# Scores of the forgetting attention in two products instead of three: queries and keys doubled in their rows, bias rows masked by head

## The chip, the cores and the metric

The kernel runs on one core of one Trainium2 chip. The metric is the device time of one execution in microseconds (us). The kernel before takes 1488.74 us, the median of three runs (1486.61 to 1490.23).

## What is computed

One layer of a decoder: a mixer of three branches (a latent attention, a forgetting attention, a state-space layer), gated and summed, and then a convolved feed-forward network, for 1024 tokens of width 1024 in float32. The change is in the forgetting attention, which has 4 heads of 64 columns. For a query i and a key j <= i its score is a product of normed rows plus a difference of running sums:

```python
q_fox = rms_norm(fq.reshape(bsz, seq, N_FOX_HEADS, FOX_HEAD_DIM), fox_q_norm_g)
k_fox = rms_norm(fk.reshape(bsz, seq, N_FOX_HEADS, FOX_HEAD_DIM), fox_k_norm_g)
log_f = jax.nn.log_sigmoid((f_logit + fox_f_bias).astype(jnp.float32))
cum_log_f = lax.cumsum(log_f, axis=1)
# in causal_block_attention, per block of 128 queries:
s = jnp.einsum('bqhd,bkhd->bhqk', qb, kb).astype(jnp.float32) * scale
s = s + (c_q - c_k)
p = jax.nn.softmax(jnp.where(mask, s, NEG_INF), axis=-1)
```

## The kernel before, in words

The program runs in four blocks: norm and input projection, `stage_fox` (this attention), `stage_mla` (the other attention), and the rest. The order on each engine is written out by hand, and semaphores join the engines. Float32 operands are multiplied in parts: each is split in a rounded high part (type fp32r) and a low part, the rest, and a product is the sum high x high, high x low, low x high, so three matrix products for one.

The projection of the gates for the third stage needs no result of the attentions, so `GateFill` spreads its 24 units of 48 products (128x512) over all stages as filling for TensorE (L540). ScalarE splits the high part of its weights (L564) and copies the results out (L575), GpSimd makes the low part (L586), once VectorE (L592), and SyncE loads and stores. In `stage_fox` the units before the first head cover the preparation: VectorE makes the running sums of log f (up to L1016), squares and norms of queries and keys (L1003 to L1027), GpSimd the power -1/2 (L955). It writes each token's 64 query or key columns and two bias columns side by side (`aug`, 66 columns): one and c for queries, -c and one for keys, so that the product over 66 rows holds the bias.

Then `Attention` runs 4 heads of 8 steps. Step i handles 128 queries against 128(i+1) keys. On TensorE (`tensor`, with `score`, `turn` and `values`) a step is:

- `score` of the step after next (L699, and L701 for the causal mask), three products for each 512 keys; it may start when ScalarE has read the same buffer (exp of this step);
- in steps 3, 5, 6 and 7, `turn` of one half of the next head's queries or keys (L685), which makes rows of the 66 columns, in a buffer of two banks;
- when the probabilities of this step are normed, their transposes (L680) into the same two banks, four blocks to a fill, with gate products between;
- every second step, `values` (L718).

A fill of a bank may begin when the low part of the fill before last is made. For each fill ScalarE writes the high part (`split_hi`, L780) and VectorE the low part (`split_lo`, L861). ScalarE also makes the exponentials (L790) and a copy of the outputs (L804), VectorE the maximum (L848), the reciprocal and the norm (L854, L856), and the sum of outputs (L867). The opening of the first head (`OPENING`) is: the two query fills, 6 gate products, the two key fills, 9 gate products, the first score.

## Time and profile before

| | us |
|---|---|
| Median of three runs (lowest to highest) | 1488.74 (1486.61 to 1490.23) |
| Span of the profiled execution, first to last instruction | 1487.9 |
| TensorE matmuls busy, of the span | 1443.8 (97%) |
| VectorE busy | 1003.4 (67%) |
| ScalarE busy | 651.2 (44%) |
| GpSimd busy | 127.2 (9%) |
| `stage_fox`, from its first gate product to its last product | about 172.7 to 343.9 |

The profiled execution has no time of its own beside its span; the span lies 0.8 us under the median. A busy TensorE is not one at its peak: matmuls overlap, their recorded length holds the latency of the array, and so what a product costs is read from the distance of starts. PEld is the weight load of TensorE, which runs beside the products. "Idle before" in a timeline row is put in brackets, with what ended it.

### The profile page before, as it was taken

Reading aid. Unit: us, or ns where it says so; the run is one execution under the profiler, and the core shown is the slowest. Engines: PE = TensorE matmul, PEld = TensorE weight load, DVE = VectorE, ACT = ScalarE, POOL = GpSimd, SP = SyncE. Lnnn points to the kernel's source line nnn. Section 1 sums busy time; section 2 is a strip of 40 time slices with the busy share of each in tenths; the row PEclk is TensorE's granted clock in tenths of the full one; section 3 lists DMA queues with packets and bytes.
Section 4 is the critical chain, followed back from the end, with each engine's and each line's share of the span. In section 5 each row is a group of like instructions: output and inputs, shape, how many; then the busy total and the mean of one; then the engine's idle time right before and its main releaser. Section 6 shows DMA issues by size and latency. Waiting matters only on the chain.

```text
span 1487.9 us, 18903 instructions
## 1 busy us (share of the span) xinstructions
PE 1443.8 (97%) x7090; PEld 1209.9 (81%) x7090; DVE 1003.4 (67%) x1378; ACT 651.2 (44%) x1054; POOL 127.2 (9%) x104
## 2 busy tenths in 40 slices
PE   7999999999999999998999999999999999999999
PEld 6999987777878777886788888888888888888887
DVE  5212366765676766856855688877877777679786
ACT  6230235554435553125632265555555555444332
POOL 1000141001420003011200000000000000000000
PEclk9999999999999999999999999999999999999999
DMA  7201231104021103226672222222222221891222
GB/s 255 67 1 75 64 92 43 37 29 147 26 84 48 33 29 100 73 64 219 211 262 85 71 62 95 85 85 79 77 86 85 85 86 49 313 388 71 85 79 78
DMA packets 129941, 148.93 MB, mean 100 GB/s; under 512 B 11002, under 2 KB 94893, under 8 KB 129581
## 3 DMA queue, kind: packets, MB, share of 16 engines
q1 hardware_dynamic: 129664, 147.67, 30.0%
q8 instruction: 56, 0.92, 0.3%
q14 instruction: 32, 0.26, 0.1%
q10 hardware_dynamic: 189, 0.08, 0.0%
HBM read 110.83 MB, written 36.31 MB: 99 GB/s over the span
## 4 chain that ended last, share of the span: by engine, by line
PE 52%; DVE 6%; issue 1%; ACT 1%; DMA 1%; POOL 0%; DVEq 0%; ACTq 0%; SPq 0%
PE ps L1876 28%; PE ps L2183 5%; PE ps L2185 5%; PE ps L2184 4%; PE ps L2753 2%; PE ps L2754 2%; PE ps L2755 2%; PE ps L540 2%; DVE plain_arena L2279 1%; PE ps L2272 1%; DMA plain_arena<-in_w_branch 1%; PE ps L2785 0%; DVE plain_arena L2543 0%; DMA plain_arena<-in_w_out 0%; DVE plain_arena L1047 0%
## 5 line engine op out<-in xcount | busy, mean ns | idle before, releaser
L1876 PE MATMUL ps<-split_arena 128*128 128x512 f32 x1320 | 306.8, 389 | 0.0
L540 PE MATMUL ps<-split_arena 128*128 128x512 f32 x1152 | 293.2, 402 | 6.0 <-PEq L1117 2.1
L1876 PEld LDWEIGHTS ps<-split_arena 128*128 128x128 f32 x1320 | 247.5, 188 | 51.4 <-issue 0.3
L540 PEld LDWEIGHTS ps<-split_arena 128*128 128x128 f32 x1152 | 210.2, 190 | 48.2 <-issue 8.2
L2059 ACT ACTIVATE down_ops<-down_all 128x1024 fp32r<-128x1024 f32 x77 | 81.5, 1061 | 115.5 <-PE ps L2185 115.3
L1876 PE MATMUL ps<-up_b,split_arena 128*128 128x512 f32 x528 | 126.5, 389 | 0.0
L2078 DVE TENSOR_TENSOR down_ops<-down_all,down_ops 128x1024 fp32r<-128x1024 f32 x77 | 94.1, 1223 | 46.2 <-ACT down_ops L2059 46.0
L2183 PE MATMUL ps<-down_ops 128*128 128x512 f32 x308 | 119.9, 389 | 0.5 <-DVE down_ops L2078 0.5
L2185 PE MATMUL ps<-down_ops 128*128 128x512 f32 x308 | 119.8, 389 | 0.0
L2184 PE MATMUL ps<-down_ops 128*128 128x512 f32 x308 | 119.8, 389 | 0.0
L1876 PEld LDWEIGHTS ps<-up_b,split_arena 128*128 128x128 f32 x528 | 99.1, 188 | 20.6
L327 PE MATMUL ps<-split_arena 128*128 128x426 f32 (+1 forms) x256 | 93.1, 364 | 2.3 <-DVE split_arena L213 2.3
L328 PE MATMUL ps<-split_arena 128*128 128x426 f32 (+1 forms) x256 | 92.0, 359 | 0.0
L329 PE MATMUL ps<-split_arena 128*128 128x426 f32 (+1 forms) x256 | 91.7, 358 | 0.0
L586 POOL TENSOR_TENSOR split_arena<-plain_arena,split_arena 128x1024 fp32r<-128x1024 f32 x23 | 63.7, 2768 | 323.2 <-ACT split_arena L564 323.2
L465 DVE COPY plain_arena<-ps 128x426 f32<-128x426 f32 (+6 forms) x28 | 10.3, 406 | 104.0 <-PE ps L329 104.0
L848 DVE TENSOR_REDUCE stat<-ps 128x1 f32<-128x128 f32 (+3 forms) x64 | 48.3, 755 | 44.2 <-PE ps L701 44.2
L2272 PE MATMUL ps<-split_arena 128*128 128x512 f32 x288 | 68.5, 394 | 6.6 <-DVE plain_arena L2279 3.7
L575 ACT ACTIVATE plain_arena<-ps 128x512 f32<-128x512 f32 x48 | 28.6, 597 | 102.7 <-DMA scr_gate<-plain_arena 68.1
L1804 DVE TENSOR_TENSOR split_arena<-up_s,split_arena 128x512 fp32r<-128x512 f32 x88 | 60.4, 687 | 18.2 <-ACT split_arena L1749 18.2
L2272 PEld LDWEIGHTS ps<-split_arena 128*128 128x128 f32 x288 | 53.4, 188 | 21.4 <-POOL split_arena L2261 8.5
L2183 PEld LDWEIGHTS ps<-down_ops 128*128 128x128 f32 x308 | 57.8, 188 | 12.7 <-DVE down_ops L2078 0.9
(359 smaller groups left out, 2510.8 us busy)
## 6 DMA issues: line engine op xcount, KB each, us to landing
plain_arena<-in_w_in SPq DMA_DIRECT2D x24, 512.0 KB, 4.2
scr_gate<-plain_arena SPq DMA_DIRECT2D x48, 256.0 KB, 2.0
plain_arena<-scr_gate SPq DMA_DIRECT2D x24, 512.0 KB, 4.3
plain_arena<-in_w_up SPq DMA_DIRECT2D x22, 512.0 KB, 5.1
up_raw<-in_w_up SPq DMA_DIRECT2D x22, 512.0 KB, 4.7
scr_act<-plain_arena SPq DMA_DIRECT2D x22, 512.0 KB, 2.7
down_all<-scr_act SPq DMA_DIRECT2D x18, 512.0 KB, 8.8
down_all<-in_w_down SPq DMA_DIRECT2D x18, 512.0 KB, 10.3
```

Of the source, the lines that this page charges most:

```text
L327: nc.tensor.matmul(o, hi, wh, start=(k == 0), stop=False)
L328: nc.tensor.matmul(o, hi, wl, start=False, stop=False)
L329: mm = nc.tensor.matmul(o, lo, wh, start=False, stop=(k == KD - 1))
L540: mm = nc.tensor.matmul(m.ps[:, self.banks[half], :], w[:, k, :], src[:, k, h * BANK:(h + 1) * BANK], start=(j == 0), stop=(j == self.PER_ ...
L586: self.m.nc.gpsimd.tensor_tensor(self.w_lo[u % 2], self.raw, f32(self.w_hi[u % 2]), ALU.subtract).then_inc(self.lo, 1)
L1876: mm = nc.tensor.matmul(o, self.w[j][w][:, k, :], self.h[j][k][h], start=(j in self.OPENS and k == 0 and n == 0), stop=(k == self.HK - 1 a ...
L2059: self.m.nc.scalar.activation(self.hi_of[n % 3], self.pair(n)[0], ACT.Copy).then_inc(self.hi, 1)
L2078: self.m.nc.vector.tensor_tensor(self.lo_of[n % 3], self.pair(n)[0], f32(self.hi_of[n % 3]), ALU.subtract).then_inc(self.lo, 1)
L2183: nc.tensor.matmul(o, a_hi[:, cut], b_hi, start=(k == 0 and j in self.OPENS), stop=False, skip_group_check=True)
L2184: nc.tensor.matmul(o, a_hi[:, cut], b_lo, start=False, stop=False, skip_group_check=True)
L2185: mm = nc.tensor.matmul(o, a_lo[:, cut], b_hi, start=False, stop=(k == HF - 1), skip_group_check=True)
L2272: mm = nc.tensor.matmul(proj_ps[u % 2][:, cut], w[:, k, :], src[:, 2 * n + k, cut], start=(k == 0 and w is hi and src is m.br_hi), stop=(k ...
```

## The change

The queries' transposed tile `q_t[0]` now holds 128 rows: the high part in rows 0 to 63 and the low part in rows 64 to 127; `k_t[0]` holds the keys' high part twice. One product over these 128 rows is high x high plus low x high. The second product, over 80 rows, is the queries' high part (`q_t[1]`, written by its own copy, L950 in the new numbering) with the keys' low part, and 16 bias rows: four for each head (ones, and the high and low part of c), the same for the queries of all heads, while those of the keys are multiplied before each head by a column that is one for the head's four rows and zero elsewhere (`head_bias`, on GpSimd). So that a transpose gives the rows twice, each token's 64 columns are written twice (`rows`, doubled by three ScalarE copies, L1061). The bias columns of all heads are transposed once, in the middle of the preparation (L1075), and four ScalarE copies put them in place (L1057). The causal mask's product stays. The other attention keeps three products. Buffers of the stage move to other addresses.

```diff
+    def score_pairs(self, tokens, keys):
+        (q_hi, q_lo), (k_hi, k_lo) = ([a[0:self.kd, cut] for a in t] for t, cut in ((self.q_t, tokens), (self.k_t, keys)))
+        return (q_hi, k_hi), (q_hi, k_lo), (q_lo, k_hi)
+
+    def ready_for_score(self, pe, h, half):
+        pe.wait_ge(self.lo, self.at["k", h, half] + 1)
...
-            for n, (x, y) in enumerate(((0, 0), (0, 1), (1, 0))):
-                nc.tensor.matmul(S[:, a:b], self.q_t[x][0:kd, i * P:(i + 1) * P], self.k_t[y][0:kd, a:b], start=(n == 0),
-                                 stop=(n == 2 and b < keys))
+            pairs = self.score_pairs(slice(i * P, (i + 1) * P), slice(a, b))
+            for n, (x, y) in enumerate(pairs):
+                nc.tensor.matmul(S[:, a:b], x, y, start=(n == 0), stop=(n == len(pairs) - 1 and b < keys))
...
-        self.ready(pe)
         for what, n in zip("qk", OPENING):
+            self.ready(pe, what)
...
+    def score_pairs(self, tokens, keys):
+        q_both, q_low = self.q_t
+        k_both, k_low = self.k_t
+        return (q_both[:, tokens], k_both[:, keys]), (q_low[0:self.LOW, tokens], k_low[0:self.LOW, keys])
+
+    def ready_for_score(self, pe, h, half):
+        pe.wait_ge(self.lo, self.at["k", h, half] + 1)
+        pe.wait_ge(self.q_kept, 2 * h + half + 1)
+        pe.wait_ge(self.bias, h + 1)
+
+    def split_hi(self, act, f):
+        x = self.fills[f]
+        if x[0] == "p":
+            super().split_hi(act, f)
+            return
+        what, h, half = x
+        cut, bank = slice(half * BANK, (half + 1) * BANK), self.m.ps[:, 4 + f % 2, :]
+        act.wait_ge(self.turned, f + 1)
+        if h:
+            act.wait_ge(self.scores, TT * (h - 1) + (4 if what == "q" and half == 0 else TT))
+        to = self.q_t if what == "q" else self.k_t
+        A = self.m.nc.scalar.activation
+        A(to[0][:, cut], bank, ACT.Copy).then_inc(self.hi, 1)
+        if what == "q":
+            A(to[1][0:FD, cut], bank[0:FD], ACT.Copy).then_inc(self.q_kept, 1)
+
+    def split_lo(self, dve, f):
+        x = self.fills[f]
+        if x[0] == "p":
+            super().split_lo(dve, f)
+            return
+        what, h, half = x
+        cut, bank = slice(half * BANK, (half + 1) * BANK), self.m.ps[:, 4 + f % 2, :]
+        dve.wait_ge(self.hi, f + 1)
+        if what == "q":
+            dve.wait_ge(self.q_kept, 2 * h + half + 1)
+            hi, lo, rows = self.q_t[0], self.q_t[0], slice(FD, 2 * FD)
+        else:
+            hi, lo, rows = self.k_t[0], self.k_t[1], slice(0, FD)
+        self.m.nc.vector.tensor_tensor(lo[rows, cut], bank[rows], f32(hi[rows, cut]), ALU.subtract).then_inc(self.lo, 1)
+
+    def head_bias(self, pool, h):
+
+        if h:
+            pool.wait_ge(self.scores, TT * h)
+        pool.wait_ge(self.fill.lo, self.fill.split)
+        r = slice(FD, self.LOW)
+        self.m.nc.gpsimd.tensor_scalar(self.k_t[1][r, :], f32(self.master[r, :]), self.of_head[r, h:h + 1], None, ALU.mult).then_inc(self.bias, 1)
+        pool.wait_ge(self.bias, h + 1)
+
+
...
-    def ready(pe):
-        pe.wait_ge(prep, 1)
+    def ready(pe, what):
+        pe.wait_ge(doubled, 1 if what == "q" else 3)
+        pe.wait_ge(bias_out, 4)
...
-            fill.gpsimd(pool, FOX_UNITS - 1)
+            mask = att.of_head
+            nc.gpsimd.memset(mask, 1.0).then_inc(const, 1)
+            pool.wait_ge(const, 4)
+            nc.gpsimd.affine_select(out=mask, in_=mask, compare_op=ALU.is_ge, fill=0.0, base=-FD, pattern=[[-4, FH]], channel_multiplier=1).then_inc(const, 1)
+            pool.wait_ge(const, 5)
+            nc.gpsimd.affine_select(out=mask, in_=mask, compare_op=ALU.is_ge, fill=0.0, base=FD + 3, pattern=[[4, FH]], channel_multiplier=-1).then_inc(const, 1)
+            fill.gpsimd(pool, FOX_PREP - 1)
+            pool.wait_ge(const, 6)
+            pool.wait_ge(bias_out, 4)
+            for h in range(H):
+                att.head_bias(pool, h)
+                fill.gpsimd(pool, 1)
...
-            fill.scalar(act, FOX_PREP * UNIT - UNIT // 2)
+            fill.scalar(act, 2 * UNIT)
+            for half in range(2):
+                cut = slice(half * BANK, (half + 1) * BANK)
+                act.wait_ge(cols_turned, half + 1)
+                for to, r in ((q_t[1], 64), (att.master, 96)):
+                    nc.scalar.activation(to[FD:FD + 16, cut], m.ps[r:r + 16, 4 + half, :], ACT.Copy).then_inc(bias_out, 1)
+            fill.scalar(act, FOX_PREP * UNIT - UNIT // 2 - 2 * UNIT)
+            for n, (first, last) in enumerate(((0, FH), (FH, FH + 1), (FH + 1, 2 * FH))):
+                act.wait_ge(prep, min(n, 1) + 1)
+                nc.scalar.activation(rows[:, :, first:last, 1, :], rows[:, :, first:last, 0, :], ACT.Copy).then_inc(doubled, 1)
             att.scalar(act)
...
-            fill.tensor(pe, (FOX_PREP - 1) * UNIT - sum(OPENING))
+            fill.tensor(pe, UNIT + UNIT // 2)
+            pe.wait_ge(cols_done, 1)
+            for t in range(TT):
+                tr = nc.tensor.transpose(m.ps[0:112, 4 + t // 4, t % 4 * P:(t % 4 + 1) * P], bias_cols[:, t, :], m.ident[:])
+                if t % 4 == 3:
+                    tr.then_inc(cols_turned, 1)
+            fill.tensor(pe, (FOX_PREP - 1) * UNIT - sum(OPENING) - UNIT - UNIT // 2)
...
-            step(V.memset(aug[:, :, 0:FH, FD:FD + 1], 1.0))
-            step(V.tensor_copy(aug[:, :, 0:FH, FD + 1], cum))
-            step(V.tensor_scalar(aug[:, :, FH:2 * FH, FD], cum, -1.0, None, ALU.mult))
-            step(V.memset(aug[:, :, FH:2 * FH, FD + 1:FD + 2], 1.0))
+            step(V.memset(bias_cols, 1.0))
+            step(V.tensor_copy(cum_hi, cum))
+            of_q, of_k = (bias_cols[:, :, at:at + 16].rearrange("p t (h n) -> p t h n", n=4) for at in (64, 96))
+            step(V.tensor_copy(of_q[:, :, :, 0], f32(cum_hi)))
+            step(V.tensor_tensor(of_q[:, :, :, 1], cum, f32(cum_hi), ALU.subtract))
+            step(V.tensor_scalar(of_k[:, :, :, 2], f32(cum_hi), -1.0, None, ALU.mult))
+            V.tensor_tensor(of_k[:, :, :, 3], f32(cum_hi), cum, ALU.subtract).then_inc(cols_done, 1)
...
-            step(V.tensor_tensor(aug[:, :, 0:FH, 0:FD], sqv[:, :, 0:FH, :],
-                                 gq.unsqueeze(1).unsqueeze(1).to_broadcast([P, TT, FH, FD]), ALU.mult))
-            V.tensor_tensor(aug[:, :, FH:2 * FH, 0:FD], sqv[:, :, FH:2 * FH, :],
+            V.tensor_tensor(rows[:, :, 0:FH, 0, :], sqv[:, :, 0:FH, :],
+                            gq.unsqueeze(1).unsqueeze(1).to_broadcast([P, TT, FH, FD]), ALU.mult).then_inc(prep, 1)
+            V.tensor_tensor(rows[:, :, FH:2 * FH, 0, :], sqv[:, :, FH:2 * FH, :],
                             gk.unsqueeze(1).unsqueeze(1).to_broadcast([P, TT, FH, FD]), ALU.mult).then_inc(prep, 1)
```

ScalarE, from the gate copies ahead of the first head to the first head's splits (`scr_gate` copies are L575; `ps` is PSUM, `split_arena` holds the split parts, `plain_arena` plain float32). Before:

```order
L575 ACTIVATE plain_arena<-ps 128x512 [waits gate_stored,gate_mm] x2
L564 ACTIVATE split_arena<-plain_arena 128x1024 [waits gate_mm,gate_w_in]
L575 ACTIVATE plain_arena<-ps 128x512 [waits gate_stored,gate_mm]
L780 ACTIVATE split_arena<-ps 66x512 [waits fox_turned] x4
L575 ACTIVATE plain_arena<-ps 128x512 [waits gate_stored,gate_mm]
```

Now:

```order
L575 ACTIVATE plain_arena<-ps 128x512 [waits gate_stored,gate_mm] x2
L564 ACTIVATE split_arena<-plain_arena 128x1024 [waits gate_mm,gate_w_in]
L575 ACTIVATE plain_arena<-ps 128x512 [waits gate_stored,gate_mm]
L1061 ACTIVATE plain_arena<-plain_arena 128x8x4x64 [waits fox_prep]
L1061 ACTIVATE plain_arena<-plain_arena 128x8x64 [waits fox_prep]
L1061 ACTIVATE plain_arena<-plain_arena 128x8x3x64 [waits fox_prep]
L948 ACTIVATE split_arena<-ps 128x512 [waits fox_turned]
L950 ACTIVATE split_arena<-ps 64x512
L948 ACTIVATE split_arena<-ps 128x512 [waits fox_turned]
L950 ACTIVATE split_arena<-ps 64x512
L948 ACTIVATE split_arena<-ps 128x512 [waits fox_turned] x2
L575 ACTIVATE plain_arena<-ps 128x512 [waits gate_stored,gate_mm]
```

Three copies of 2048, 512 and 1536 columns stand between the last gate copy and the first split, and each query split is two instructions.

TensorE, the opening of the first head, as a difference (- before, + now):

```order
-L685 MATMUL ps<-ident,plain_arena 66x128 [waits fox_prep]
-L685 MATMUL ps<-ident,plain_arena 66x128 x7
+L686 MATMUL ps<-ident,plain_arena 128x128 [waits fox_bias_out,fox_doubled]
+L686 MATMUL ps<-ident,plain_arena 128x128 x7
 L540 MATMUL ps<-split_arena 128x512 x6
-L685 MATMUL ps<-ident,plain_arena 66x128 [waits fox_lo]
-L685 MATMUL ps<-ident,plain_arena 66x128 x3
-L685 MATMUL ps<-ident,plain_arena 66x128 [waits fox_lo]
-L685 MATMUL ps<-ident,plain_arena 66x128 x3
+L686 MATMUL ps<-ident,plain_arena 128x128 [waits fox_lo,fox_bias_out,fox_doubled]
+L686 MATMUL ps<-ident,plain_arena 128x128 x3
+L686 MATMUL ps<-ident,plain_arena 128x128 [waits fox_lo]
```

The transposes give 128 rows, those of the queries wait for the first doubling copy and those of the keys for the third, and nothing between them moved.

ScalarE, steps 4 and 5 of the first head, where the second query half of the next head is split (`fox_pt` is the transposed probabilities). Before:

```order
L804 ACTIVATE plain_arena<-ps 64x512 [waits fox_pv]
L780 ACTIVATE split_arena<-ps 66x512 [waits fox_scores,fox_turned]
L780 ACTIVATE fox_pt_1385<-ps 128x4x128 [waits fox_pv,fox_turned]
L780 ACTIVATE fox_pt_1385<-ps 128x2x128 [waits fox_pv,fox_turned]
L790 ACTIVATE plain_arena,stat<-ps,stat 128x1024 [waits fox_recip,fox_turned,fox_negmax]
```

Now:

```order
L812 ACTIVATE plain_arena<-ps 64x512 [waits fox_pv]
L948 ACTIVATE split_arena<-ps 128x512 [waits fox_scores,fox_turned]
L950 ACTIVATE split_arena<-ps 64x512
L788 ACTIVATE fox_pt_1386<-ps 128x4x128 [waits fox_pv,fox_turned]
L788 ACTIVATE fox_pt_1386<-ps 128x2x128 [waits fox_pv,fox_turned]
L798 ACTIVATE plain_arena,stat<-ps,stat 128x1024 [waits fox_recip,fox_turned,fox_negmax]
```

The copy of the queries' high part (L950) stands between the split of the query fill and that of the probabilities.

## Rows read from the trace of the kernel before

**Rows 1.** The page: the span, and each engine's busy time and instructions.
```profile
span 1487.9 us, 18903 instructions
...
PE 1443.8 (97%) x7090; PEld 1209.9 (81%) x7090; DVE 1003.4 (67%) x1378; ACT 651.2 (44%) x1054; POOL 127.2 (9%) x104
```

**Rows 2.** By stretch: length, busy PE, PEld, DVE, ACT, POOL, granted clock, DMA share, GB/s.
```profile
172.00:219.00 47.00, 46.70 (x217) 38.59 (x216) 31.62 (x54) 15.98 (x21) 20.32 (x7) 1.00 0.36 107
219.00:343.00 124.00, 119.33 (x729) 97.39 (x728) 81.77 (x166) 68.03 (x148) 9.61 (x4) 1.00 0.12 37
```

**Rows 3.** Timeline of PE, second head: start, length, line, out<-in, shape, count.
```profile
253.41 0.91 PE L699 MATMUL ps<-split_arena 66*128 66x512 f32 x3
254.16 0.23 PE L701 MATMUL ps<-maskb,identb 128*128 128x128 bf16 x1
...
255.85 1.15 PE L699 MATMUL ps<-split_arena 66*128 66x512 f32 x6
256.83 0.23 PE L701 MATMUL ps<-maskb,identb 128*128 128x128 bf16 x1
...
266.93 1.61 PE L699 MATMUL ps<-split_arena 66*128 66x512 f32 x6
268.38 0.23 PE L701 MATMUL ps<-maskb,identb 128*128 128x128 bf16 x1
...
276.66 0.49 PE L699 MATMUL ps<-split_arena 66*128 66x128 f32 x3
```

**Rows 4.** Timeline of PE, last gate products before the first head.
```profile
204.63 9.46 PE L540 MATMUL ps<-split_arena 128*128 128x512 f32 x41
213.93 1.04 PE L685 MATMUL ps<-ident,plain_arena 128*66 128x128 f32 x8
...
219.13 0.45 PE L699 MATMUL ps<-split_arena 66*128 66x128 f32 x3
```

**Rows 5.** Timeline of ACT, first stage and opening of the first head.
```profile
178.00 3.63 ACT L964 ACTIVATE plain_arena<-plain_arena 128x4096 f32<-128x4096 f32 x1 [0.88 <-DMA scr_u<-plain_arena]
181.53 2.17 ACT L966 ACTIVATE split_arena<-plain_arena 128x512 fp32r<-128x512 f32 x4
...
213.07 0.60 ACT L575 ACTIVATE plain_arena<-ps 128x512 f32<-128x512 f32 x1 [1.16 <-DMA scr_gate<-plain_arena]
...
214.56 1.08 ACT L780 ACTIVATE split_arena<-ps 66x512 fp32r<-66x512 f32 x2 [0.90 <-PE ps L685]
```

**Rows 6.** Timeline of ACT, steps 0 and 1 of the second head.
```profile
253.67 0.28 ACT L780 ACTIVATE fox_pt<-ps 128x128 fp32r<-128x128 f32 x1 [3.01 <-PE ps L718]
...
255.48 0.60 ACT L804 ACTIVATE plain_arena<-ps 64x512 f32<-64x512 f32 x1
```

**Rows 7.** Timeline of PEld, step 2 of the second head.
```profile
257.65 0.31 PEld L680 LDWEIGHTS ps<-ident,plain_arena 128*128 128x128 f32 x3 [0.50 <-DVE plain_arena L856]
```

**Rows 8.** Timelines of ACT, DVE and PE, steps 5 and 6 of the second head.
```profile
269.08 0.60 ACT L780 ACTIVATE split_arena<-ps 66x512 fp32r<-66x512 f32 x1 [0.96 <-PE ps L685]
...
269.79 0.68 DVE L861 TENSOR_TENSOR split_arena<-ps,split_arena 66x512 fp32r<-66x512 f32 x1
...
272.14 1.02 DVE L861 TENSOR_TENSOR fox_pt<-ps,fox_pt 128x512 fp32r<-128x512 f32 x2
...
272.88 0.63 PE L685 MATMUL ps<-ident,plain_arena 128*66 128x128 f32 x4 [0.86 <-DVE fox_pt L861]
```

**Rows 9.** POOL, groups of the whole span, shapes apart: count, busy us, mean ns.
```profile
L586 POOL TENSOR_TENSOR split_arena<-plain_arena,split_arena 128x1024 fp32r<-128x1024 f32 x23 | 63.7, 2768 | 323.2 <-ACT split_arena L564 323.2
...
L955 POOL TENSOR_TENSOR statb<-stat,plain_arena 128x64 f32<-128x64 f32 x1 | 10.9, 10933 | 8.2 <-DVE stat L1004 8.2
```

**Rows 10.** Timelines of DVE and POOL in the preparation of the first attention.
```profile
203.27 4.37 DVE L1025 TENSOR_TENSOR plain_arena<-plain_arena,rowg 128x2048 f32<-128x2048 f32 x1
207.67 2.29 DVE L1027 TENSOR_TENSOR plain_arena<-plain_arena,rowg 128x2048 f32<-128x2048 f32 x1
...
201.55 3.94 POOL L586 TENSOR_TENSOR split_arena<-plain_arena,split_arena 128x1024 fp32r<-128x1024 f32 x1 [2.77 <-ACT split_arena L564]
```

## Prediction of the time after the change

> **What bounds the kernel now.** I read the page first: TensorE's products are busy 97% of the span, the next engine 67% [rows 1]. The stretches of this stage say the same at the full clock: 46.70 of 47 us in the preparation, 119.33 of 124 in the four heads, where VectorE has 81.77 and ScalarE 68.03 [rows 2]. So the stage lasts as long as TensorE's queue, and time taken from it comes back unless something ends a wait there later. TensorE's recorded lengths overlap, so its small waits hide in "busy": I went through one head in the timelines and looked for places where it is held by another engine. There are two kinds: in step 2 its weight load waits 0.50 us for the norm [rows 7], and before the key fill of step 6 it waits 0.86 us for a low part of probabilities [rows 8]. What a third product less returns depends on whether it stands behind the event that starts such a chain, or within it.
>
> **What is removed.** 48 products, one of three for each 512 keys or fewer. The three cost, from first start to the mask's start, 1.45 us at 3 x 1024 columns, 0.98 us at 3 x 640 and 0.75 us at 3 x 512 [rows 3]: 0.47 to 0.51 ns a column. A head has 4608 key columns, so a head saves between 2.17 and 2.35 us, taken as 2.23, by step 0 to 7: 0.06, 0.13, 0.19, 0.25, 0.33, 0.37, 0.42, 0.48. Four heads: 8.9 us. The new products have 128 and 80 rows where the old have 66. The gate products have 128 rows and 512 columns, and 41 of them start within 9.30 us, 0.227 us each [rows 4], no more than the 0.23 to 0.24 of the old ones; rows cost nothing. The Trainium skill speaks against this in "TensorE: Matmul & The Clock Gate", Part 3, The mechanism: a weight load overlaps a running product only when their row groups differ. By that rule each product of 128 rows would pay its load as well. The gate products all use the same 128 rows and still keep 0.227 us, so the trace disagrees, and the measurement decides.
>
> **What is added before the first head.** Eight transposes of 112 columns on TensorE, 0.10 us each by the eight of the first query fills, 1.04 us with the last one's latency of 0.27 [rows 4]: 0.8 us. Four copies of 16x512 on ScalarE, at 0.54 us (two splits in 1.08 us [rows 5]) 2.2 us, while ScalarE is busy 15.98 of 47 us [rows 2] and stands waiting for the store of the gates; hidden. The longer VectorE part (a fill of 896 columns and two more small operations, 0.7 to 1.4 us) fits in what VectorE has free (31.62 of 47 us busy [rows 2]; it waits for GpSimd's power), and GpSimd's mask column is three small operations; both hidden. The gate split that VectorE makes is late by as much, with a bound of 0.9 us if it carries through the loads to ScalarE's last gate copy.
>
> Not hidden is the doubling. It stands on ScalarE behind the gate copy at 213.07 [rows 5], and I let that copy start 0.2 later for the eight transposes, 213.27. Then, step by step: the copy 0.54; three copies of 4096 columns together at the price of the square of 4096, 3.63 [rows 5], and two more starts, 0.2: 217.6. The queries' first split and its new twin 1.08: 218.7. VectorE's low part 0.7 [rows 8]: 219.4; meanwhile the second half's split and twin end at 219.8, its low part at 220.5. The second key fill is turned after that, 4 x 0.11: 220.95. Nine gate products 9 x 0.227: 223.0, and 0.2 for the hand-overs: the first score starts at 223.2 instead of 219.13 [rows 4]. **The start costs 4.1 us.** Below it lies 2.6, if the doubling overlaps half with the 6 and 9 gate products; above it 8.8, if copies in pieces of 64 columns cost twice a plain row (+3.8) and the 0.9 of the loads comes on top.
>
> **What is added in the heads.** The twin copy of each query half, 0.54 us on ScalarE, stands between split and low part. In step 3 it moves the low part of the fill, the norm and the next transposes, which TensorE reaches just as late: 0. In step 5 it counts. Take the end of the score of step 7, about 268.6, as origin: the split starts at +0.5 (269.08), the low part at +1.2 (269.79), the low part of the probabilities at +3.5 (272.14), and TensorE waits for it until +4.3 (272.88, 0.86 idle) [rows 8]. VectorE works through from the one to the other. With the twin the low part starts at +1.6, so TensorE goes on at +4.7: 0.42 us lost in heads 0 to 2, none in head 3, which prepares no next head. Bounds: 0, and 0.54 at both halves.
>
> GpSimd's bias product for the next head may start when step 7's score is done, 268.61, and is needed at the next head's first score, 276.66 [rows 3]: 8.05 us of cover. No row shows a GpSimd product with a scalar. The nearest is the low part of 1024 columns, 2.40 us where nothing disturbs it (2.77 on the mean [rows 9]), and I take that: 0. The upper end is the power, 10.93 us for 64 columns [rows 9]. Two more waits before each score cost nothing while TensorE's queue is ahead.
>
> **What of the 8.9 us comes back.** In the heads with an output copy at step 1 (1 to 3) a chain starts when `values` has ended, 253.6: ScalarE's split of step 0 at 253.67, the gate weights, the exp, the output copy at 255.48 [rows 6], VectorE's sum and the norm (L856), and only then TensorE's transposes at 257.65, for which it waits 0.50 [rows 7]. Scores of steps 3 and 4 (0.25 and 0.33) run beside this chain: lost. So is step 1 (0.13), which stands before a key fill that VectorE holds. Steps 0, 2, 5, 6 and 7 lie before the origins of the chains and move them: 0.06 + 0.19 + 0.37 + 0.42 + 0.48 = 1.52. Less the twin: 1.10 for heads 1 and 2, 1.52 for head 3. Head 0 has no output copy at step 1 and keeps 0.58 more: 1.68. Sum 1.68 + 2.20 + 1.52 = 5.4 us.
>
> **The sum.** 5.4 - 4.1 = 1.3 us less than the profiled span: 1486.6 of 1487.9. The median of the runs lies 0.8 above that span, so I forecast 1487.4 us. A difference under 0.2%, 3.0 us, can't be told from no change here.
>
> **Rivals.**
> - *All of it comes back.* TensorE's 97% speaks for it; the waits of 0.50 and 0.86 us against. If the chains shrink with the products and the twin is covered: 8.9 - 4.1 = 4.8, 1483.9 us. Chance 0.22.
> - *The start costs its upper end.* The doubling runs in 64-column pieces and ScalarE's gate copy comes late. For it: everything there hangs on one engine in order. Against: the square runs on plain rows at 0.89 ns a column, and the splits of the values, which are 512 columns in pieces of 64, take 0.54 us each (four in 2.17 [rows 5]), as one of plain rows. 8.8 instead of 4.1: 1492.1. It turns the sign over 0.2% from a start of 8.4 on. Chance 0.11.
> - *GpSimd's bias product is slower than its cover* (slower than before). Place: between the last score of a head and the first of the next. At the power's 10.93 us each of three heads waits 2.9 us: 8.6 us, 1496.0. It decides from 8.05 us on. Against it: an elementwise operation of 1024 columns took 2.4. A weaker form needs only 2.8 us: while GpSimd reads, VectorE's operations with both inputs in SBUF stand still. This case shows it: the key and the query rows are the same product of 2048 columns, 2.29 us alone and 4.37 with GpSimd's low part beside it, which itself took 3.94 [rows 10]. VectorE's operations in the 2.8 us after the score read PSUM. That is how the Trainium skill has it ("SBUF — State Buffer", Who interferes with whom: an exclusive lock, taken by two SBUF inputs and not by one), and the trace agrees with the lock. Chance 0.05.
> - *Two products last as long as three*, because 128 rows cost more than 66. Then only the costs stay: 4.1 + 3 x 0.42 = 5.4 us, 1494.1. Rows 4 speak against it. Chance 0.03.
>
> **Numbers.** The forecast has 0.59. The range takes in the first rival with a little spread, and most of the way to the second: 1483.4 to 1491.2; 0.1 lies on each side. Faster by over 0.2%, below 1485.8: the 0.22 and a tail of the forecast (a start of 2.6 gives 1485.9), 0.27. Slower, above 1491.7: the last three rivals without the mild half of the second, 0.14. The same: 0.59.
>
> **What would show it.** After: first score about 4 us later against the start of the stage; three copies of 3.8 us in all on ScalarE ahead of it; scores of step 7 at 0.97 us to the mask; the four heads together about 5 us shorter than their 124; the wait of step 2 grown from 0.5 to about 1.1 us, the one of step 6 from 0.86 to about 1.3; the bias product near 2.4 us. I am wrong if step 2's wait has not grown, if the start is off by over 1 us, or if the time moved outside this stage.

## The result, and the profile after

| | before | after |
|---|---|---|
| Median of the runs (lowest to highest) | 1488.59 us (1486.61 to 1490.23, 5) | 1494.91 us (1493.63 to 1496.82, 5) |
| Ratio, with its 95% interval | | 1.0044 (1.0033 to 1.0055) |
| Span of the profiled execution (its own time after: 1494.63) | 1487.9 us | 1492.9 us |
| Start: stage's first long gate group to first score | 43.65 us | 51.86 us |
| Heads: first score to the gate products behind the last head | 123.64 us | 120.80 us |
| From there to the end of the span | 1145.1 us | 1145.4 us |

The change made the kernel slower, by 0.33 to 0.55%. The forecast was 1487.4 us, a tie, in a range up to 1491.2; it was wrong. In the profiles the time moved only inside this stage (8.2 - 2.8 = 5.4 us of it; the rest is within 0.6 us), and both terms of the sum are off in the same direction: the start costs 8.2 us where 4.1 were forecast, and the heads return 2.8 us where 5.4 were. "Start" and "heads" are used in this sense from here on.

The page after the change, the lines that answer to [rows 1]:

```profile
span 1492.9 us, 18903 instructions
...
PE 1438.4 (96%) x7050; PEld 1203.0 (81%) x7050; DVE 1004.7 (67%) x1380; ACT 660.6 (44%) x1069; POOL 143.8 (10%) x111
```

TensorE lost 40 instructions (48 products less, 8 transposes more) and 5.4 us of busy time, and the span grew by 5.0. The busy time of GpSimd grew by 16.6 us. By stretch, after (length, busy PE, PEld, DVE, ACT, POOL, clock, DMA share, GB/s), for [rows 2]:

```profile
172.00:227.00 55.00, 48.90 (x226) 38.86 (x224) 30.77 (x56) 23.03 (x31) 30.25 (x11) 1.00 0.30 91
227.00:348.00 121.00, 112.73 (x679) 89.95 (x679) 82.65 (x166) 70.79 (x154) 18.07 (x7) 1.00 0.12 38
```

Before, TensorE had 0.3 us free in the preparation; now 6.1, at a granted clock of 1.00 in both. So the start isn't slower products but waiting. TensorE's timeline shows where (start, length, line, shapes, count, and in brackets the wait before it):

```profile
174.88 8.86 PE L540 MATMUL ps<-split_arena 128*128 128x512 f32 x38 [0.29 <-PEq L265]
...
209.41 8.06 PE L540 MATMUL ps<-split_arena 128*128 128x512 f32 x33 [2.04 <-POOL split_arena L586]
219.57 1.09 PE L686 MATMUL ps<-ident,plain_arena 128*128 128x128 f32 x8 [2.10 <-ACT plain_arena L1061]
220.42 1.64 PE L540 MATMUL ps<-split_arena 128*128 128x512 f32 x6
223.31 0.63 PE L686 MATMUL ps<-ident,plain_arena 128*128 128x128 f32 x4 [1.25 <-DVE split_arena L965]
...
226.74 0.33 PE L708 MATMUL ps<-split_arena 128*128 128x128 f32 x2
```

First 2.04 us for GpSimd's low part of a gate weight, which nobody had to wait for before; then 2.10 us for the doubling; then 1.25 us for the opening's low parts, behind the copies of the queries.

Why GpSimd is late stands in its own timeline, after, with VectorE's of the same time. They answer to [rows 10]:

```profile
198.12 0.10 POOL L1031 MEMSET cidx<- 128x4 f32 x1
198.29 4.39 POOL L1033 TENSOR_SCALAR_AFFINE_SELECT cidx<-cidx 128x4 f32<-128x4 f32 x1
202.75 2.26 POOL L1035 TENSOR_SCALAR_AFFINE_SELECT cidx<-cidx 128x4 f32<-128x4 f32 x1
204.97 4.39 POOL L586 TENSOR_TENSOR split_arena<-plain_arena,split_arena 128x1024 fp32r<-128x1024 f32 x1
```

```profile
198.20 4.43 DVE L1126 TENSOR_TENSOR plain_arena<-plain_arena,statb 128x4096 f32<-128x4096 f32 x1 [2.96 <-POOL statb L1029]
202.66 2.29 DVE L1128 TENSOR_TENSOR plain_arena<-plain_arena,rowg 128x2048 f32<-128x2048 f32 x1
204.87 2.28 DVE L1130 TENSOR_TENSOR plain_arena<-plain_arena,rowg 128x2048 f32<-128x2048 f32 x1
```

Two selects over 4 columns took 4.39 and 2.26 us, and each ends when a VectorE product with two SBUF inputs ends: 198.20 + 4.43 = 202.63 against 202.68, 202.66 + 2.29 = 204.95 against 205.01. Then the low part of 1024 columns waits out the third product and is ready at 209.36; before it was ready at 205.49, since it came behind one product only [rows 10]. The stores and loads that hang on the gate products move with it, and with them ScalarE's gate copies, from 213.07 [rows 5] to 217.12 (4.65 us later, counted from the stage's first long gate group). ScalarE, after:

```profile
214.41 0.60 ACT L575 ACTIVATE plain_arena<-ps 128x512 f32<-128x512 f32 x1 [9.64 <-DMA scr_gate<-plain_arena]
...
217.12 0.60 ACT L575 ACTIVATE plain_arena<-ps 128x512 f32<-128x512 f32 x1 [1.17 <-DMA scr_gate<-plain_arena]
217.62 3.80 ACT L1061 ACTIVATE plain_arena<-plain_arena 128x2048 f32<-128x2048 f32 x3
221.31 0.58 ACT L948 ACTIVATE split_arena<-ps 128x512 fp32r<-128x512 f32 x1
221.79 0.58 ACT L950 ACTIVATE split_arena<-ps 64x512 fp32r<-64x512 f32 x1
```

In the heads, the distance from one causal mask product (L701, L709 after) to the next on TensorE says what a step takes. Interval k ends at the mask of step k; 0 is the boundary, from step 7 of the head before. For the second head, in us:

| kernel | 0 | 1 | 2 | 3 | 4 | 5 | 6 | 7 |
|---|---|---|---|---|---|---|---|---|
| before | 8.25 | 0.48 | 3.79 | 4.23 | 2.67 | 3.65 | 3.55 | 4.35 |
| after | 9.14 | 0.36 | 3.76 | 4.23 | 2.39 | 3.85 | 3.15 | 4.17 |
| before, low x high left out | 8.14 | 0.37 | 3.72 | 4.19 | 2.38 | 3.78 | 3.15 | 3.89 |
| after, three moves | 8.42 | 0.37 | 3.75 | 4.19 | 2.39 | 3.86 | 3.15 | 3.88 |

The last two rows are of experiments below (6 and 4). A score is issued two steps ahead, so interval 7 holds TensorE's work of step 4, and the boundary that of steps 5 and 6. After the change intervals 4, 6 and 7 are shorter, 5 and above all the boundary are longer.

### The profile page after: what moved, and what is told of

It is laid out like the page before. It is cut to its first block, busy times and chain, and to the rows that moved or that the text cites. A ratio compares the mean times of both kernels' runs of the same rounds, so it can differ in the third digit from the quotient of the medians.

```text
span 1492.9 us, 18903 instructions
## 1 busy us (share of the span) xinstructions
PE 1438.4 (96%) x7050; PEld 1203.0 (81%) x7050; DVE 1004.7 (67%) x1380; ACT 660.6 (44%) x1069; POOL 143.8 (10%) x111
## 4 chain that ended last, share of the span: by engine, by line
PE 52%; DVE 6%; issue 1%; ACT 1%; DMA 1%; POOL 0%; DVEq 0%; ACTq 0%
PE ps L1979 28%; PE ps L2286 5%; PE ps L2288 5%; PE ps L2287 4%; PE ps L2858 2%; PE ps L2856 2%; PE ps L2857 2%; PE ps L540 2%; DVE plain_arena L2382 1%; PE ps L2375 1%; DMA plain_arena<-in_w_branch 1%; PE ps L2888 0%; DVE plain_arena L2646 0%; DVE plain_arena L1150 0%; ACT plain_arena L2358 0%
## 5 line engine op out<-in xcount | busy, mean ns | idle before, releaser
L575 ACT ACTIVATE plain_arena<-ps 128x512 f32<-128x512 f32 x48 | 28.6, 597 | 101.3 <-DMA scr_gate<-plain_arena 63.6
```

## The experiments

Each "moved early" or "later" below is the kernel after the change with that one thing moved, and "start" and "heads" are of its profiled execution. They were run in three groups of four on one chip each; the kernel before had medians of 1488.22 (experiments 1 to 3 and the first run of 4), 1487.99 (6 to 8 and the first of 9) and 1487.39 us (the others) beside them. Each ratio is against those runs, as it stands on record; it isn't the quotient of the two medians (in experiment 5 that would be 1.0008 instead of 1.0001).

Costs are read from start and heads, not from the times of whole runs. Two profiles of one kernel (experiment 4) agree within 0.02 us in both, while from the heads' end on the profiles of all these kernels last 1143.4 to 1148.3 us, where the code is the same in all but the two with a later split in both attentions. TensorE's granted clock goes with that. It falls from 1.00 to 0.50 (2.4 to 1.2 GHz) for about 3 us at two to four places of each profile (its very end left out), mostly behind this stage: from 400 to 700 us it is 0.97, 0.98 and 0.98 by 100 us in experiment 1, which has the 1148.3, and 0.98, 1.00 and 1.00 in experiment 3, which has the 1143.4. In 89 runs of the kernel before the median is 1486.9 us at a mean clock of 0.999 (48 runs), 1488.2 at 0.998 (20) and 1489.1 at 0.997 (17). The kernels of the experiments have mean clocks of 0.996 to 0.998 beside 0.998 of the kernel before, and their medians lie 0.4 to 2.8 us above what start and heads say. Why their clock falls more often is not shown.

**1. The mask column, made before GpSimd waits for its gate piece.**

```diff
+            mask = att.of_head
+            nc.gpsimd.memset(mask, 1.0).then_inc(const, 1)
...
+            nc.gpsimd.affine_select(out=mask, in_=mask, compare_op=ALU.is_ge, fill=0.0, base=FD + 3, pattern=[[4, FH]], channel_multiplier=-1).then_inc(const, 1)
             fill.gpsimd(pool, 1)
             pool.wait_ge(ms_done, 1)
             nc.gpsimd.tensor_tensor(rstd, ssq, expo, ALU.pow).then_inc(rstd_done, 1)
-            mask = att.of_head
...
```

> The changed kernel with GpSimd's three operations that make the mask column (a fill and two selects of 128x4) moved ahead of the power, into GpSimd's idle time. 'Start' is from the stage's first gate product to the first score: 43.65 us before, 51.86 in the changed kernel. Theory (the two selects meet VectorE's products of 4096 and 2048 columns, last 4.39 and 2.26 us for 4 columns each and hold GpSimd's low part back): selects under 0.5 us each, low part of the gates done near 205.5 us, start 51.9 - 3.9 = 48.0 us, heads unchanged at 120.8; time 1491.0 us. Rival (the start is late because VectorE's part has a fill of 896 columns and carries through the loads, or because of the doubling alone): start stays over 51 us, time 1494.9 us.

Measured: start 47.64 us, 4.2 less; heads 120.69; 1491.41 us, ratio 1.0025 (1.0013 to 1.0037). The selects took 0.23 and 0.19 us there, and the low part is back in its old place, beside one product:

```profile
202.74 2.71 POOL L586 TENSOR_TENSOR split_arena<-plain_arena,split_arena 128x1024 fp32r<-128x1024 f32 x1 [4.01 <-ACT split_arena L564]
```

So half of the start's cost is the place of two operations of 0.2 us, as expected (48.0 us). What is left of it, 47.64 - 43.65 = 4.0 us, is what the forecast had.

**2. The doubling, ahead of ScalarE's last gate piece.** The loop over `doubled` (L1061) goes from behind the last gate copies to behind the first of them, where ScalarE waits for a store.

```diff
-            fill.scalar(act, FOX_PREP * UNIT - UNIT // 2 - 2 * UNIT)
+            fill.scalar(act, UNIT // 2)
             for n, (first, last) in enumerate(((0, FH), (FH, FH + 1), (FH + 1, 2 * FH))):
...
+            fill.scalar(act, FOX_PREP * UNIT - UNIT - 2 * UNIT)
             att.scalar(act)
```

> The changed kernel with the three doubling copies put ahead of ScalarE's last two gate copies, where it waits 9.64 us for a store; the mask column stays where it is. Theory (the doubling is wholly on the path because it stands behind the last gate copy): it ends before that copy, start 51.9 - 3.8 = 48.1 us; time 1491.1 us. Rival (TensorE's opening is held by the chain split, twin, low part, turn, and would wait there anyway): start shorter by less than 2 us, time over 1493 us.

Measured: start 49.90 us, 2.0 less; heads 120.72; 1493.08 us, ratio 1.0035 (1.0022 to 1.0047). The copies themselves lie in a wait of ScalarE now, and TensorE's wait of 2.05 us for GpSimd stands as before. ScalarE then waits for the transposes of the first turn:

```profile
216.69 0.60 ACT L575 ACTIVATE plain_arena<-ps 128x512 f32<-128x512 f32 x1 [1.17 <-DMA scr_gate<-plain_arena]
218.97 0.60 ACT L948 ACTIVATE split_arena<-ps 128x512 fp32r<-128x512 f32 x1 [1.68 <-PE ps L686]
```

The figure of 2.0 us can't be taken as it is. The 33 gate products ahead of the turn took 9.42 us here and 8.06 in the changed kernel, since the granted clock was 0.81 from 210 to 211 us and 0.50 from 211 to 214:

```profile
209.07 9.42 PE L540 MATMUL ps<-split_arena 128*128 128x512 f32 x33 [2.05 <-POOL split_arena L586]
```

TensorE goes from them to the turn without a wait, so 1.36 us of the start are this fall of the clock. Without it the start would be about 48.5 us and the move worth 3.3 (an estimate from these two rows): nearly the 3.8 of the theory, and not the rival, whose terms (under 2 us, over 1493 us) the measured values meet. Before the fall TensorE had waited 2.05 us and worked again for 1 to 2 us; the changed kernel's wait of 2.04 us was followed by none (1.00 from 172 to 227).

**3. The copy of the queries, behind the low parts.** It is made from the high part in SBUF, after the next fill of probabilities, and VectorE's low part no longer waits for it.

```diff
         if what == "q":
-            A(to[1][0:FD, cut], bank[0:FD], ACT.Copy).then_inc(self.q_kept, 1)
+            self.pending.append((f, cut))
+        elif h == 0 and half == 1:
+            self.keep_q(act)
...
         if what == "q":
-            dve.wait_ge(self.q_kept, 2 * h + half + 1)
             hi, lo, rows = self.q_t[0], self.q_t[0], slice(FD, 2 * FD)
```

> The changed kernel in which the second copy of the queries' high part is read from SBUF behind the next fill's split, and VectorE's low part no longer waits for it. 'Heads' is from the first score to the stage's last gate products: 123.6 us before, 120.8 in the changed kernel, where 8.9 us of products went. Theory (the twin is what took most of the gain, 1.1 us in each of three heads): heads 117.5 us, start shorter by 0.5 to 1.1 us; time 1490.7 us. Rival (the chains through exp, sum and norm keep the time of the products whatever the twin does): heads 119.5 us or more, only the 0.42 us of each head that I had given the twin come back; time 1493 us.

Measured: start 51.01, heads 118.50 us, 2.3 less; 1490.92 us, ratio 1.0025 (1.0016 to 1.0035). The heads lie 1.0 us over the expected 117.5 and below the rival's 119.5. The clock fell in the opening here too (0.66 from 209 to 214 us), but TensorE still waited 0.80 us for the doubling behind it, so the start doesn't hold that.

**4. All three moves.** No diff of its own; run twice.

> The three edits together. Theory (three separate costs that add up): the doubling now meets the gate copies and leaves 1.5 to 2.5 us of the start, so start 46 us, heads 117.5 us; 2.3 more and 6.1 less than the kernel before: 1484.8 us. Rival (one store or load paces the start whatever ScalarE and GpSimd do, and the chains pace the heads): start 48 or more and heads 119.5 or more, 1489 us.

> The same kernel as all_three, to stand beside the next one on one chip. Start 45.0 us, heads 118.4 us, ratio about 0.998 to the kernel before, 1485.2 us. If it is a tie instead, the gain of the change with its costs moved away is under what five rounds can tell.

Measured: start 45.02 and 45.00, heads 118.45 and 118.46; 1485.24 us, ratio 0.9984 (0.9968 to 0.9999), and 1485.17 us, 0.9983 (0.9974 to 0.9992). With its costs moved, the change gains 0.17%, less than the 0.2% that the text took as the bound of what can be told, but with both intervals below 1. TensorE passes the opening without a wait:

```profile
204.66 10.59 PE L540 MATMUL ps<-split_arena 128*128 128x512 f32 x46
215.09 1.03 PE L686 MATMUL ps<-ident,plain_arena 128*128 128x128 f32 x8
...
220.29 0.33 PE L708 MATMUL ps<-split_arena 128*128 128x128 f32 x2
```

From the first turn to the first score it takes 5.20 us, as in the kernel before (213.93 to 219.13 [rows 4]). The 1.35 us that stay lie ahead of the turn. Of them 0.8 are the eight added transposes; most of the other 0.5 stands before the gate products that need VectorE's low part (L592): it starts 1.25 us later than before against the stage's first long gate group, and two products that were 0.23 us apart are 0.52 apart there.

**5. Mask and doubling moved, the copy of the queries left.**

> The mask column and ScalarE's doubling both stand ahead of GpSimd's and ScalarE's first gate pieces; the copy of the queries to the second half stays where the change put it. Theory: with the two selects off VectorE's products, the three doubling copies (3.8 us) again stand between ScalarE's last gate copy and its first turn, so taking them away as well gives nearly all of them back: start about 45.3 us (45.02 with all three moves; 47.64 with the mask alone), heads unchanged at 120.7, so about 1487.5 us, a tie with the kernel before. Rival: TensorE's transposes bound the start, so the doubling gives 2 us again as it did alone (49.90 from 51.86) and the start is 45.7 or more. Second rival: the copy of the queries costs the start 0.8 us as in the kernel before with that copy alone; then 45.8 to 46.2.

Measured: start 45.90, heads 120.74 us; 1488.56 us, ratio 1.0001 (0.9992 to 1.0011). The second rival held: the copy costs 45.90 - 45.00 = 0.9 us in the start and 120.74 - 118.46 = 2.3 us in the heads, and those 3.2 us are the whole distance to the kernel of experiment 4 and turn its gain into a tie. Of the 2.3 us, 0.8 lie in interval 7 of the first three heads (0.29, 0.25 and 0.25: the copy in step 3) and 1.45 in the three boundaries (0.72, 0.37 and 0.36: the copy in step 5). Without GpSimd's lateness the doubling was worth 47.64 - 45.90 = 1.7 us on the path, not its 3.8, since ScalarE would else have stood there for TensorE. The granted clock in the stage's opening was 1.00 in both.

**6. The kernel before with two products.** The product low x high is left out in this attention (the queries' low part isn't used), and nothing is added.

```diff
-            for n, (x, y) in enumerate(((0, 0), (0, 1), (1, 0))):
+            for n, (x, y) in enumerate(((0, 0), (0, 1), (1, 0))[:self.products]):
```

> The kernel before with only the first two of the three products of each score of the forgetting attention (low x high is left out, the output differs); nothing is added anywhere. It measures what the 48 products are worth here. 'Heads' is from the first score to the stage's last gate products: 123.6 us before. The products are 8.9 us. Theory (chains through ScalarE and VectorE that start when the values have ended, or when a low part is made, keep part of it whatever else is done): heads 118.4 us, as the 118.45 of the three edits together; time 1483 us. Rival (the products' 8.9 us come back and the rest is lost to twins and bias products): heads 115 to 116 us, time 1480 us.

Measured: start 43.63, heads 117.75 us; 1483.28 us, ratio 0.9971 (0.9957 to 0.9984). This is what the removed products are worth with nothing to pay: 5.9 us of the 8.9 that they last, read from the stage; the ratio of whole runs gives 4.3 (2.4 to 6.4).

**7. The kernel before with the mask column alone**, in the place where the change makes it; its result isn't used.

```diff
             nc.gpsimd.tensor_tensor(rstd, ssq, expo, ALU.pow).then_inc(rstd_done, 1)
+            mask = m.cidx[:, 0:FH]
+            nc.gpsimd.memset(mask, 1.0).then_inc(const, 1)
...
             fill.gpsimd(pool, FOX_UNITS - 1)
```

> The kernel before with nothing but GpSimd's three operations of 128x4 for the mask column, at the place where the changed kernel has them (their result is not used). Theory (each select waits out one of VectorE's products, then the low part of the gates waits out the third): the selects last over 2 us each, start (43.65 us before) 46.5 to 47.5 us, heads unchanged, time 1492 us. Rival (they are long only beside the other changes of the preparation): start unchanged, time 1488.5 us.

Measured: start 45.42 (+1.8, less than the 2.9 to 3.9 expected), heads 124.39 (+0.75, nearly all in interval 2 of the first head, 2.04 us for 1.32); 1491.51 us, ratio 1.0024 (1.0014 to 1.0034). The selects stretch alike, but here the low part came in ahead of the third product, and VectorE waited instead. GpSimd and VectorE in this kernel:

```profile
198.56 4.39 POOL L959 TENSOR_SCALAR_AFFINE_SELECT cidx<-cidx 128x4 f32<-128x4 f32 x1
203.02 2.25 POOL L961 TENSOR_SCALAR_AFFINE_SELECT cidx<-cidx 128x4 f32<-128x4 f32 x1
205.24 2.36 POOL L586 TENSOR_TENSOR split_arena<-plain_arena,split_arena 128x1024 fp32r<-128x1024 f32 x1
```

```profile
202.93 2.29 DVE L1031 TENSOR_TENSOR plain_arena<-plain_arena,rowg 128x2048 f32<-128x2048 f32 x1
205.26 4.49 DVE L1033 TENSOR_TENSOR plain_arena<-plain_arena,rowg 128x2048 f32<-128x2048 f32 x1
```

The low part started 0.02 us ahead of the product here and ran undisturbed, 2.36 us; in the changed kernel it started 0.10 us behind it and took 4.39. About a tenth of a microsecond decides 2 us.

**8. The kernel before with the copy of the queries alone**, into rows that nothing reads.

```diff
+        if x[0] == "q" and self.twin is not None:
+            self.m.nc.scalar.activation(hi, src, ACT.Copy)
+            self.m.nc.scalar.activation(self.twin[0:FD, x[2] * BANK:(x[2] + 1) * BANK], src[0:FD], ACT.Copy).then_inc(self.hi, 1)
+            return
```

> The kernel before with nothing but a second copy of 64 rows of each query fill on ScalarE, into unused space, for which VectorE's low part waits. Theory (0.5 us on a chain in two places of three heads): heads 123.6 + 1.5 to 2.3 = 125.1 to 125.9 us, start + 0 to 0.5; time 1490.5 us. Rival (TensorE has enough work here to cover it, it costs only where the products have gone): heads 124 us at most, time 1488.8 us.

Measured: start 44.43 (+0.8), heads 124.87 (+1.2, between the theory's 1.5 and the rival's 0.4); 1490.54 us, ratio 1.0016 (1.0004 to 1.0028). All of the 1.2 us lies in the three boundaries: 8.66, 9.03 and 8.65 us instead of 8.25, 8.62 and 8.25, that is 0.41, 0.41 and 0.40, to set against the 0.42 of the forecast. With three products the copy in step 3 costs nothing and that in step 5 1.2 us; with two the same copies cost 0.8 and 1.45, together 2.3. Where the 0.8 come from is seen in step 4 of the second head (interval 7). The changed kernel, VectorE and TensorE's weight load:

```profile
268.85 0.69 DVE L965 TENSOR_TENSOR split_arena<-ps,split_arena 64x512 fp32r<-64x512 f32 x1 [0.66 <-ACT split_arena L950]
...
269.78 0.55 DVE L864 TENSOR_SCALAR plain_arena<-plain_arena,stat 128x640 f32<-128x640 f32 x1
```

```profile
270.12 0.10 PEld L709 LDWEIGHTS ps<-maskb,identb 128*128 128x128 bf16 x1 [0.15 <-issue]
270.38 0.42 PEld L681 LDWEIGHTS ps<-ident,plain_arena 128*128 128x128 f32 x4 [0.17 <-DVE plain_arena L864]
```

VectorE waits 0.66 us for the copy (L950), so its norm (L864) ends at 270.33, after TensorE's score. In the kernel before with the copy alone, the norm is ready at 264.44 and TensorE's score, with its third product, ends only behind the mask at 264.86:

```profile
263.89 0.55 DVE L861 TENSOR_SCALAR plain_arena<-plain_arena,stat 128x640 f32<-128x640 f32 x1
```

```profile
264.86 0.23 PE L702 MATMUL ps<-maskb,identb 128*128 128x128 bf16 x1
264.92 0.61 PE L681 MATMUL ps<-ident,plain_arena 128*128 128x128 f32 x4
```

In step 4 a product that the change removes was what hid the copy that it adds. The same goes on at the boundary, where the changed kernel's TensorE waits for the low part of the queries and then for that of the probabilities (first head's end, start and wait):

```profile
246.23 0.44 PE L681 MATMUL ps<-ident,plain_arena 128*128 128x128 f32 x2 [0.49 <-DVE split_arena L965]
248.34 0.66 PE L686 MATMUL ps<-ident,plain_arena 128*128 128x128 f32 x4 [0.73 <-DVE fox_pt L869]
```

**9. ScalarE's gate split of step 0, issued behind the output copy of step 1.** Added to experiment 4; first in this attention, then in both.

```diff
+            if i == 1 and isinstance(self, BiasedAttention):
+                self.fill.scalar(act, ATT_FILL[0])
...
-            if not first:
+            if not first and not (i == 0 and isinstance(self, BiasedAttention)):
                 self.fill.scalar(act, ATT_FILL[i])
```

> The version with the three edits, and ScalarE's split of the gate weights moved from between the split of step 0's probabilities and the exp of step 2 to behind the output copy of step 1. If the chain from the end of the values over split, gate split, exp, output copy, sum and norm to the transposes of step 2 is what keeps the products of steps 3 and 4, its 1.05 us go from the chain: the wait before the transposes of step 2 (0.6 us on TensorE) goes in three heads, heads 118.45 - 1.8 = 116.7 us, time 1483.3 us against 1485.2. Rival (another wait is next at the same place, or the low part of the gates then comes beside the norm): heads 118 us or more.

> all_three, with ScalarE's gate split of step 0 issued behind step 1's output copy in both attentions of the program. Theory: TensorE's wait of 0.8 to 1.05 us in step 2 is ScalarE's queue, so it goes in both attentions: this stage's heads 117.1 us again (start 45.0), the second attention's heads also shorter, by 0.5 to 1.8 us, and 1482.5 to 1484 us. Rival: what the split frees in step 2 comes back as another wait (VectorE's product behind GpSimd's, seen in head 2 of this attention), and the second attention gains nothing: 1484.5 to 1485.5, a tie with all_three.

Measured, this attention: start 45.04, heads 117.11; span 1481.1, but a median of 1485.65 us, ratio 0.9988 (0.9973 to 1.0002). Both: heads 117.03; 1483.70 us, ratio 0.9973 (0.9964 to 0.9983), the lowest of all runs that leave nothing of the computation out. In the second attention interval 5 of three heads falls from 3.62 to 3.35 us, 0.8 in all; its length as a whole (112.89 us for 113.68) is no measure, since the two profiles of experiment 4 have 112.15 and 113.68 there, with the difference in one interval (2.29 and 3.84 us), over which the clock had fallen in the second. It is not shown that it beats experiment 4: the two intervals of the ratio overlap, and the median with the split later in this attention alone (1485.65) is no lower than experiment 4's. What is shown is the mechanism: step 2's wait is ScalarE's queue and GpSimd's place. With the three moves, the weight load waits 1.06 us in step 2 of the second head; with the split later it has no wait there. ScalarE and VectorE in step 1, three moves:

```profile
253.14 1.05 ACT L564 ACTIVATE split_arena<-plain_arena 128x1024 fp32r<-128x1024 f32 x1
254.09 0.57 ACT L798 ACTIVATE plain_arena<-ps,stat 128x384 f32<-128x384 f32 x1
...
254.78 0.60 ACT L812 ACTIVATE plain_arena<-ps 64x512 f32<-64x512 f32 x1
```

```profile
255.41 0.68 DVE L875 TENSOR_TENSOR plain_arena<-ps,plain_arena 64x512 f32<-64x512 f32 x1 [1.23 <-ACT plain_arena L812]
...
256.19 0.75 DVE L864 TENSOR_SCALAR plain_arena<-plain_arena,stat 128x384 f32<-128x384 f32 x1
```

and with the split later in both, VectorE:

```profile
255.43 0.42 DVE L866 TENSOR_SCALAR plain_arena<-plain_arena,stat 128x384 f32<-128x384 f32 x1
...
257.26 1.13 DVE L866 TENSOR_SCALAR plain_arena<-plain_arena,stat 128x512 f32<-128x512 f32 x1
```

The rival was right in part: in the third head GpSimd's low part, now 1.3 us later in its head, meets a VectorE product with two SBUF inputs (L884), which takes 1.60 instead of 0.67 us, and interval 6 is 3.91 us instead of 3.15; in the first head a norm takes 2.12 us, and interval 5 is 3.38 instead of 3.00.

**10. The later split in the kernel before**, in both attentions.

> The kernel before with only the later gate split, in both attentions; nothing of the change is in it. Theory: step 2's wait of 0.50 us goes in heads 1 to 3, so heads of this stage 122.1 (from 123.6), start 43.65, the second attention alike, and about 1486 us. Rival: that wait is bounded by VectorE's low part by then and not by ScalarE's queue, so nothing is gained: heads 123.6, 1488.5 us. If it wins as much as in the changed kernel, the later split is independent of the change.

Measured: start 43.64, heads 123.04, 0.6 less, not 1.5; 1487.23 us, ratio 0.9999 (0.9990 to 1.0008): no difference that can be told. In the second to fourth head interval 5 falls from 3.65, 3.61 and 3.62 to 3.36 and 3.35 twice, 0.8 us in all, but in the first head interval 2 grows from 1.32 to 1.53. The later split is worth more in the changed kernel (1.4 us against 0.6), where step 2's wait is longer.

## Why the prediction was wrong, step by step

- The account in one line: of 6.7 us between forecast and stage, 4.1 are the start, nearly all the mask column, and 2.6 the heads: 0.8 for the products, 1.0 for the copy of the queries, 0.7 open.
- **The start: the step that failed is the sentence "GpSimd's mask column is three small operations; both hidden".** It was put at nothing because it is small. It stands on an engine whose next work, the gate low part, TensorE needs, and it was put beside three VectorE products with two SBUF inputs each. [rows 10] showed the very effect, a low part of 3.94 us beside such a product, and the text even explained it by the Trainium skill ("SBUF — State Buffer", Who interferes with whom: the engine that issues first holds the shared ports for the whole instruction, and the other is blocked). It applied that to the bias product and not here. By that rule each of the two selects waits for the end of the running product; the trace agrees, 4.39 and 2.26 us for 0.2. Experiment 1 puts the price at 4.2 us.
- **The rest of the start was right in its sum by luck: its terms cancel.** Without the lock it costs 4.0 us, with 4.1 forecast. The doubling took 3.80 us, as worked out (3.8), but is worth 1.7 on the path, since TensorE's part of the chain was late by itself: 1.35 us lie ahead of the first turn, where the chain of the forecast, which followed ScalarE alone, had 0.2. Some 0.5 of them come through VectorE's late gate split, which the forecast had as hidden with a bound of 0.9. The copy of the queries is worth 0.9; 0.54 stood in the chain for it.
- **What the products return was a little too high.** The forecast before the copy's cost is 6.7 us; experiment 6 has 5.9. The terms of the last steps hold: in the second head intervals 6 and 7 fell by 0.40 and 0.46, for 0.42 and 0.48. So the step that was mis-sized is the middle of a head: steps 1 to 5 were to give 0.56 us (steps 2 and 5), and in heads 1 to 3 intervals 1 to 5 fell by 0.36. The chain of step 2, thought to run through the output copy and VectorE's sum, ended on a norm that waits for GpSimd (below); that this keeps the rest is argued, not shown.
- **The copy of the queries in the heads: right in the kernel that was costed, wrong in the changed one.** The forecast put the copy in step 3 at 0, since TensorE reaches what waits for it "just as late", and that in step 5 at 0.42 in each of three heads. Both are exact where three products stay (experiment 8: 0, and 0.40 to 0.41). With two they are 0.8 and 1.45 us (experiments 4 and 5), 2.3 for 1.3. The step that failed is the 0 of step 3: to take the cover of an added cost from the profile before, when the change removes part of that cover. It was reckoned against one row of the old timeline, with origin at the end of a score of three products.
- The heads in one line: -5.9 for the products, +0.7 for what differs between that kernel and the three moves, +2.3 for the copy: -2.9; measured -2.84. The 0.7 (mostly boundaries 0.28, 0.03 and 0.28 us longer and interval 5 by 0.07 in three heads) stays open; no run took it apart.
- **The bias product** took 2.84 us each time, not 2.4, and started on the end of the head's last score, as said; nothing is seen to wait for it. Two products of 128 and 80 rows cost what two of three did: the score of step 7 takes 0.98 us to its mask with the three moves, for 0.97. Those two rivals are excluded.
- Of the signs named, "the start is off by over 1 us" came true, by 4.1; the four heads are 2.8 us shorter, not 5. The three copies took 3.8, and step 2's wait grew from 0.50 to 1.05 us, as forecast (1.1). It is the weight load's row, for [rows 7]:

```profile
264.49 0.31 PEld L681 LDWEIGHTS ps<-ident,plain_arena 128*128 128x128 f32 x3 [1.05 <-DVE plain_arena L864]
```

and step 6's stayed at 0.88 (0.86 before) where 1.3 was forecast (for [rows 8]), because the copy's delay shows one row earlier, in the weight load's wait for the transposes:

```profile
276.92 0.20 PEld L681 LDWEIGHTS ps<-ident,plain_arena 128*128 128x128 f32 x2 [0.57 <-DVE split_arena L965]
```

```profile
279.17 0.66 PE L686 MATMUL ps<-ident,plain_arena 128*128 128x128 f32 x4 [0.88 <-DVE fox_pt L869]
```

- The rival "the start costs its upper end" gave 1492.1 us with a start of 8.8. The size was nearly that (8.2), its reasons were not: the copies in pieces of 64 columns cost what plain rows cost, and the gate copy came late by 4.65 us against the stage's first gate group, not by 0.9, and 4.2 of that from GpSimd, not from VectorE's split (in experiment 1 it is 0.44 late).

## What to carry to other kernels

Cost an operation on GpSimd by what VectorE runs at that moment, not by its size: a select over 4 columns took as long as the two-input product beside it, and moving it by a few lines gave 4.2 us. When a change removes work from the engine that bounds, go through each added cost again with the shorter timeline, since the removed work may have been its cover: the same two copies cost 1.2 us with three products and 2.3 with two. And measure the removal alone: the product's 8.9 us were worth 5.9.

## What the runs showed of the hardware that was not expected

- The lock between GpSimd and VectorE also holds for a VectorE operation with one tensor from SBUF. The norm (a tensor times a column, SBUF to SBUF) took 0.42 us for 384 columns where it started ahead of GpSimd's low part, 0.75 where GpSimd's low part still ran for 0.5 us, 1.28 us in the first head of the changed kernel, and 1.13 instead of 0.49 for 512 columns. GpSimd and VectorE there, changed kernel:

```profile
230.31 2.40 POOL L586 TENSOR_TENSOR split_arena<-plain_arena,split_arena 128x1024 fp32r<-128x1024 f32 x1 [8.84 <-ACT split_arena L564]
```

```profile
231.65 1.28 DVE L864 TENSOR_SCALAR plain_arena<-plain_arena,stat 128x384 f32<-128x384 f32 x1
```

  In all 24 norms of step 2 in six profiles (the kernels before and after, experiments 1 and 6, both runs of 4) the norm began during the low part and ended 0.21 to 0.22 us behind its end. The prediction had it that one SBUF input takes no lock. The same section of the Trainium skill names the two-port mode of VectorE as a second case that takes the pair; that this norm runs in that mode is an inference from its waits and its length, which grows by 0.07 us for 128 columns (0.42, 0.49 and 0.55 us for 384, 512 and 640), half of what the two-input product takes a column (2.29 us for 2048). It puts about 0.3 us of step 2's wait of 1.05 us on GpSimd's place rather than on ScalarE's queue.
- GpSimd's product with a column took 2.84 us for 16x1024 in fp32r, longer than its difference of two full tensors of 128x1024 (2.40 us undisturbed). An eighth of the partitions didn't make it the cheaper of the two; whether the type, the column or the rows that start at 64 cost the rest was not tried.
